# Two transformer blocks on one core: value rows centred before retention, the last down tile stacked in two parts, semaphores cleared in ranges

## The reference, cut to what matters

```python
def swiglu_ffn(x, w13, w2):
    a, u = jnp.split(x @ w13, 2, axis=-1)      # 2 x 2752 columns
    return (jax.nn.silu(a) * u) @ w2           # 2752 rows -> 1024

def retention(q, k, v, g, gn_g):               # 4 heads of 128, chunk-causal with decay
    ...
    mu = jnp.mean(o, axis=-1, keepdims=True)
    var = jnp.mean(jnp.square(o - mu), axis=-1, keepdims=True)
    o = ((o - mu) * lax.rsqrt(var + LN_EPS)).transpose(0, 2, 1, 3).reshape(B, L, D_RET) * gn_g
    return (jax.nn.silu(g.astype(f32)) * o).astype(g.dtype)

for l in range(DEPTH_2):
    h = layer_norm(DEEPNORM_ALPHA * h + 0.5 * swiglu_ffn(h, ffn1...), ...)
    mix = token_mix(h, w_in[l], ...)           # pooling, convolution, retention, then w_out
    h = layer_norm(DEEPNORM_ALPHA * h + mix, ...)
    h = layer_norm(DEEPNORM_ALPHA * h + 0.5 * swiglu_ffn(h, ffn2...), ...)
```

## Time and profile before

| | us |
|---|---|
| Runs shown (3) | 3224.69, 3225.98, 3226.51; median 3225.98 |
| The profiled execution | 3223.9, span 3222.1 |
| TensorE busy | 3138.6 (97%), granted clock 0.992 of full speed |
| VectorE, ScalarE, GpSimd busy | 973.9, 869.7, 1072.2 |
| "layers" begins | 1164.1 |
| Down products of the last group, first FFN of layer 0, begin | 1519.3 |
| Values of layer 0's mixer | 1658.4 to 1686.9 |
| Mixer's tail, layer 0 | 1719.2 to 1766.3 |
| Mixer's tail, layer 1 | 2737.5 to 2784.6 |

### The profile page before, as it was taken

How to read it: one execution, slowest core, us unless ns; L and a number is a source line. 1 busy time by engine, 2 the same in 40 slices (tenths; PEclk the granted TensorE clock), 3 DMA queues, 4 the chain that set the end, 5 groups by cost and what they waited for, 6 DMA issues and landing times.

```text
span 3222.1 us, 54521 instructions
## 1 busy us (share of the span) xinstructions
PE 3138.6 (97%) x23934; PEld 2553.9 (79%) x23934; DVE 973.9 (30%) x1762; ACT 869.7 (27%) x1304; POOL 1072.2 (33%) x563
## 2 busy tenths in 40 slices
PE   7999999989999989999999999999999999999998
PEld 3465578544444469999998999999999999888886
DVE  3144765531211241111463311113111254421113
ACT  2042423110000052222523522125221243252223
POOL 1030266200000034333563433344333355354442
PEclk9999999999999989999999999999999999999999
DMA  7541000349999942222221222222222222112220
GB/s 316 204 133 53 27 3 3 133 203 428 429 428 429 428 167 92 79 105 74 91 79 53 73 99 79 95 83 79 99 102 76 92 80 79 53 66 105 105 95 30
DMA packets 37752, 438.86 MB, mean 136 GB/s; under 512 B 5910, under 2 KB 6678, under 8 KB 11542
## 3 DMA queue, kind: packets, MB, share of 16 engines
q1 hardware_dynamic: 36088, 434.24, 34.2%
q10 hardware_dynamic: 1444, 1.36, 0.2%
HBM read 432.70 MB, written 2.10 MB: 135 GB/s over the span
## 4 chain that ended last, share of the span: by engine, by line
PE 62%; DVE 1%; ACT 0%; DVEq 0%; issue 0%; ACTq 0%
PE PS L2635 42%; PE PS L2632 11%; PE PS L2644 3%; PE PS L2909 2%; PE PS L2280 1%; PE PS L2942 1%; PE PS L2286 1%; PE PS L2927 1%; PE PS L2643 1%; PE PS L2293 0%; PE PS L2904 0%; DVE high L2385 0%; PE PS L2951 0%; DVE high L3229 0%; DVEq L2454 0%; DVE low L3223 0%
## 5 line engine op out<-in xcount | busy, mean ns | idle before, releaser
L2622 POOL TENSOR_TENSOR w_lo<-low,w_hi 128x2048 fp32r<-128x2048 f32 (+2 forms) x206 | 744.1, 3617 | 1565.5 <-ACT w_hi L2617 1565.1
L2635 PE MATMUL PS<-h_hi,w_hi 128*128 128x264 f32 x2656 | 553.8, 286 | 3.5 <-DVE h_lo L3254 3.4
L2635 PE MATMUL PS<-h_lo,w_hi 128*128 128x264 f32 x2656 | 552.1, 285 | 0.0
L2635 PE MATMUL PS<-h_hi,w_lo 128*128 128x264 f32 x2656 | 551.6, 285 | 0.0
L2617 ACT ACTIVATE w_hi<-low 128x2048 fp32r<-128x2048 f32 (+2 forms) x206 | 312.1, 1524 | 459.1 <-PE PS L2635 367.4
L2635 PEld LDWEIGHTS PS<-h_hi,w_hi 128*128 128x128 f32 x2656 | 417.3, 188 | 7.2 <-issue 6.2
L2635 PEld LDWEIGHTS PS<-h_lo,w_hi 128*128 128x128 f32 x2656 | 416.3, 188 | 0.0
L2635 PEld LDWEIGHTS PS<-h_hi,w_lo 128*128 128x128 f32 x2656 | 415.8, 188 | 0.0
L2772 DVE TENSOR_TENSOR low<-low,PS 128x528 f32<-128x528 f32 (+1 forms) x84 | 58.8, 699 | 778.0 <-PE PS L2635 556.3
L2635 PE MATMUL PS<-g_hi,w_hi 128*128 128x264 f32 x1056 | 231.9, 286 | 0.0
L2635 PE MATMUL PS<-g_hi,w_lo 128*128 128x264 f32 x1056 | 230.4, 285 | 0.0
(11 more groups left out here) (402 smaller groups left out, 4617.4 us busy)
## 6 DMA issues: line engine op xcount, KB each, us to landing
arena<-wts_dram SPq DMA_DIRECT2D x108, 2048.0 KB, 18.1
low<-wts_dram SPq DMA_DIRECT2D x70, 2048.0 KB, 7.7
arena<-wmod_dram SPq DMA_DIRECT2D x9, 2048.0 KB, 8.7
low<-wts_dram SPq DMA_DIRECT2D x12, 1536.0 KB, 6.4
arena<-na_bias_dram SPq DMA_DIRECT2D x16, 512.0 KB, 3.5
arena<-x_dram SPq DMA_DIRECT2D x2, 2048.0 KB, 8.2
high<-tab_dram SPq DMA_DIRECT2D x1, 2225.0 KB, 25.2
low<-wts_dram SPq DMA_DIRECT2D x2, 1024.0 KB, 5.1
```

The source lines that it names most:

```text
L2622: nc.gpsimd.tensor_tensor(lo, raw, hi.bitcast(F32), ALU.subtract).then_inc(w_l.sem, 1)
L2635: mm = nc.tensor.matmul(bank(b, h), w[wi], halves(x[xi])[:, h, :], start=(first and i == 0), stop=(last and i == 2))
```

## The change

Three edits. First, `clear` sorts the semaphore numbers and clears each consecutive run of them in one instruction; the order of instructions then has one clear at each of the three places instead of 50, 99 and 48.

Second, the last down tile is stacked. The host puts the 64 real rows a second time on partitions 64 to 127. GpSimd overwrites the last 128 columns of w_hi there with the low part of the weights (raw minus rounded), between two drains, and makes w_lo only for the other 896 columns. VectorE makes g on both halves of the partitions (a second multiply of 64 partitions, after a drain). The down products of this tile have two passes instead of three.

Third, the mean over a head's 128 values is taken from the values, not from the outputs: ScalarE evicts each value unit in two halves of 128 columns (one head each) with the sum over the columns as a second output, VectorE subtracts the mean from the value tile (`value_centre`, behind the convolution), and `values` waits for the centred tiles. `group_mean` and `group_centre` go; ScalarE squares the output straight from PSUM ahead of its copy. The tail's order is rewritten.

```diff
     def clear(self, sp):
-        for s in self.held:
-            sp.sem_clear(s)
+        at = sorted(s.num for s in self.held)
+        for i, n in enumerate(at):
+            if not i or at[i - 1] != n - 1:
+                first = n
+            if i + 1 == len(at) or at[i + 1] != n + 1:
+                sp.sem_clear(range(first, n + 1))
...
     def split_pool(pool, l, i):
         _, raw, hi, lo = piece(i)
         w_h.wait(pool, l, i + 1)
+        if i % NS in LAST_DOWN:
+            n, r = (GROUPS[-1][1] - 1) * P, slice(P // 2, P)
+            nc.gpsimd.drain()
+            nc.gpsimd.tensor_tensor(hi[r, n:], raw[r, n:], hi[r, n:].bitcast(F32), ALU.subtract)
+            nc.gpsimd.drain()
+            raw, hi, lo = raw[:, 0:n], hi[:, 0:n], lo[:, 0:n]
         nc.gpsimd.tensor_tensor(lo, raw, hi.bitcast(F32), ALU.subtract).then_inc(w_l.sem, 1)
+    LAST_DOWN = [w * S_FFN2 + S_FFN - DK + m for w in range(2) for m in range(DK)]
...
+    STACKED = ((0, 0), (0, 1))
...
-                                   range(2) if h is None else (h,))
+                                   range(2) if h is None else (h,), **(dict(pairs=STACKED) if f0 + f == FT - 1 else {}))
...
-                    x, r = gs[0:64, f % 2, :], slice(0, 64)
-                    nc.vector.tensor_tensor(toks(x, fin), toks(gs[64:128, f % 2, :], fin), sums(4, fin)[64:128], ALU.mult).then_inc(g_sb.sem, 1)
+                    x = gs[:, f % 2, :]
+                    nc.vector.tensor_tensor(toks(x[0:64], fin), toks(x[64:128], fin), sums(4, fin)[64:128], ALU.mult)
+                    nc.vector.drain()
+                    nc.vector.tensor_tensor(toks(x[64:128], fin), toks(x[64:128], fin), sums(4, fin)[64:128], ALU.mult).then_inc(g_sb.sem, 1)
...
             elif kind == "v":
-                c = 256 * (t // 5)
-                nc.scalar.activation(v[:, t % 5, c:c + 256], PS[:, b, 0:256], ACT.Copy).then_inc(u_a.sem, 1)
+                for x in range(2):
+                    at = 256 * (t // 5) + P * x
+                    nc.scalar.activation(v[:, t % 5, at:at + P], PS[:, b, P * x:P * x + P], ACT.Copy,
+                                         accum_out=vsum[:, 2 * t + x:2 * t + x + 1])
+                nc.scalar.drain().then_inc(u_a.sem, 1)
...
         def head_out(h):
             ro_ps.wait(act, l, h + 1)
+            if h >= 2:
+                gv_ps.wait(act, l, h - 1)
+            nc.scalar.activation(halves(sq2[h % 2]), PS[:, 4:6, 0:LH], ACT.Square).then_inc(gq_sb.sem, 1)
             nc.scalar.activation(halves(qT[:, h, :]), PS[:, 4:6, 0:LH], ACT.Copy).then_inc(ro_sb.sem, 1)
...
+        def value_centre(t):
+            taken(dve, l, "v", t)
+            x = v[:, t % 5, 256 * (t // 5):256 * (t // 5) + 256].rearrange("p (h n) -> p h n", h=2)
+            nc.vector.scalar_tensor_tensor(x, vsum[:, 2 * t:2 * t + 2].unsqueeze(2).to_broadcast([P, 2, P]), -1.0 / P, x,
+                                           ALU.mult, ALU.add).then_inc(vc_sb.sem, 1)
...
         convolve(len(taps))
+        for t in range(10):
+            value_centre(t)
...
+            m[DFF:] = m[DFF - P // 2:DFF]
```

More of the change, by code:

```diff
@@ L2190, in second_block @@
     u = M3.take(2, CW - 1 + L)
+    vsum = M3.take(20)
     acc, ropet, csq = (hT[:, 2 * i:2 * i + 2, :] for i in range(3))
@@ L2626, in weights, with product @@
         return piece(i)[2:]
-    def product(b, w, x, first, last, fin=False, hs=range(2)):
-        for i, (wi, xi) in enumerate([(0, 0), (0, 1), (1, 0)]):
+    def product(b, w, x, first, last, fin=False, hs=range(2), pairs=((0, 0), (0, 1), (1, 0))):
+        for i, (wi, xi) in enumerate(pairs):
+            ends = dict(start=(first and i == 0), stop=(last and i == len(pairs) - 1))
             if fin:
-                mm = nc.tensor.matmul(PS[:, b, :], w[wi], x[xi][:, NMETA:], start=(first and i == 0), stop=(last and i == 2))
+                mm = nc.tensor.matmul(PS[:, b, :], w[wi], x[xi][:, NMETA:], **ends)
                 continue
             for h in hs:
-                mm = nc.tensor.matmul(bank(b, h), w[wi], halves(x[xi])[:, h, :], start=(first and i == 0), stop=(last and i == 2))
+                mm = nc.tensor.matmul(bank(b, h), w[wi], halves(x[xi])[:, h, :], **ends)
         return mm
+    STACKED = ((0, 0), (0, 1))
     def first_three(pe, l, uu, i, fin=False):
@@ L2770, in ffn_dve @@
                 if f < FT - 1:
[L2771 removed]
+                    x = gs[:, f % 2, :]
                     nc.vector.tensor_tensor(toks(x, fin), toks(x, fin), sums(4 * (f % 2) + 2, fin), ALU.mult).then_inc(g_sb.sem, 1)
                 else:
[L2774 to L2775 removed]
+                    x = gs[:, f % 2, :]
+                    nc.vector.tensor_tensor(toks(x[0:64], fin), toks(x[64:128], fin), sums(4, fin)[64:128], ALU.mult)
+                    nc.vector.drain()
+                    nc.vector.tensor_tensor(toks(x[64:128], fin), toks(x[64:128], fin), sums(4, fin)[64:128], ALU.mult).then_inc(g_sb.sem, 1)
                 gh_sb.wait(dve, l, n + 1)
[L2777 removed]
+                nc.vector.tensor_tensor(toks(g_lo[:, f - f0, :], fin), toks(x, fin), toks(g_hi[:, f - f0, :].bitcast(F32), fin), ALU.subtract).then_inc(gl_sb.sem, 1)
             def evacuate(m, h=None, apart=4):
@@ L2837, in second_block @@
     st_ps, st_sb, ro_ps, ro_sb = Sig("st_ps", 4 * RH), Sig("st_sb", 4 * RH), Sig("ro_ps", RH), Sig("ro_sb", RH)
-    gm_ps, gc_sb, gq_sb, gv_ps, ge, gr, gi, gb_ps, gz, gy_sb = (Sig(x, RH) for x in (
-        "gm_ps", "gc_sb", "gq_sb", "gv_ps", "ge", "gr", "gi", "gb_ps", "gz", "gy_sb"))
+    gq_sb, gv_ps, ge, gr, gi, gb_ps, gz, gy_sb = (Sig(x, RH) for x in (
+        "gq_sb", "gv_ps", "ge", "gr", "gi", "gb_ps", "gz", "gy_sb"))
+    vc_sb = Sig("vc_sb", 10)
     wo_ps, wo_sb = Sig("wo_ps", NU_LN), Sig("wo_sb", NU_LN)
@@ L2933, in values @@
                 ro_sb.wait(pe, l, h)
+                gq_sb.wait(pe, l, h)
             else:
                 taken(pe, l, "pool", 1)
+            vc_sb.wait(pe, l, 5 + 5 * (h // 2))
             for hf in range(2):
@@ L2944, in values, with group_var @@
             last.then_inc(ro_ps.sem, 1)
-        def group_mean(h):
-            ro_sb.wait(pe, l, h + 1)
+        def group_var(h):
+            gq_sb.wait(pe, l, h + 1)
             if h >= 2:
                 gz.wait(pe, l, h - 1)
-            for hf in range(2):
-                last = nc.tensor.matmul(bank(GN_BANK[h], hf), C["mean_h"], halves(qT[:, h, :])[:, hf, :], start=True, stop=True)
-            last.then_inc(gm_ps.sem, 1)
-        def group_var(h):
-            gq_sb.wait(pe, l, h + 1)
             quads(GN_BANK[h], 0, sq2[h % 2], True, True, "mean_h").then_inc(gv_ps.sem, 1)
@@ L2984, in mix_pe @@
         st_sb.wait(pe, l, 4 * RH)
-        group_mean(1)
+        group_var(1)
+        out_part(0, range(0, 2))
         values(3)
-        group_mean(2)
-        group_var(1)
-        out_part(0, range(0, 4))
+        group_spread(1)
         group_var(2)
-        group_spread(1)
+        out_part(0, range(2, 4))
+        group_var(3)
         ro_sb.wait(pe, l, RH)
         out_part(1, range(0, 2))
-        group_mean(3)
         group_spread(2)
         out_part(1, range(2, 4))
-        group_var(3)
+        group_spread(3)
         for m in range(2):
             out_part(m, (4, 5))
-        group_spread(3)
         for k in (6, 7):
@@ L3062, in head_out @@
             ro_ps.wait(act, l, h + 1)
+            if h >= 2:
+                gv_ps.wait(act, l, h - 1)
+            nc.scalar.activation(halves(sq2[h % 2]), PS[:, 4:6, 0:LH], ACT.Square).then_inc(gq_sb.sem, 1)
             nc.scalar.activation(halves(qT[:, h, :]), PS[:, 4:6, 0:LH], ACT.Copy).then_inc(ro_sb.sem, 1)
-        def group_square(h):
-            gc_sb.wait(act, l, h + 1)
-            nc.scalar.activation(sq2[h % 2], qT[:, h, :], ACT.Square).then_inc(gq_sb.sem, 1)
         def group_root(h):
@@ L3086, in mix_act @@
         head_out(2)
-        group_square(1)
+        group_root(1)
         head_out(3)
-        group_square(2)
-        group_root(1)
         group_root(2)
         mixed_hi(4)
-        group_square(3)
-        mixed_hi(5)
         group_root(3)
-        mixed_hi(6)
-        mixed_hi(7)
+        for k in range(5, DK):
+            mixed_hi(k)
         for i in range(2, 6):
@@ L3211, in decayed @@
                 last.then_inc(st_sb.sem, 1)
-        def group_centre(h):
-            gm_ps.wait(dve, l, h + 1)
-            nc.vector.tensor_tensor(halves(qT[:, h, :]), halves(qT[:, h, :]), bank(GN_BANK[h]), ALU.subtract).then_inc(gc_sb.sem, 1)
         def group_eps(h):
@@ L3247, in mix_dve @@
         group_inverse(2)
-        group_centre(3)
+        group_eps(3)
         group_scale(2)
-        group_eps(3)
         group_inverse(3)
```

11 lines of the change are left out of this document (1 added, 10 removed).

## The result

| | before | after |
|---|---|---|
| median of the runs | 3226.24 us (3224.69 to 3226.93, 4 runs) | 3204.74 us (3202.56 to 3206.22, 4 runs) |
| profiled execution, its span | 3223.9, 3222.1 us | 3205.7, 3203.8 us |

The ratio is 0.9937 (95% interval 0.9924 to 0.9949): 21.5 us less by the medians, 18.3 by the two spans. Forecast were 3206.6 us and 19.4 us less. Later the changed kernel was timed again: 3204.71 us over 5 runs, ratio 0.994 (0.9927 to 0.9954), 19.5 us under the 3224.21 of the kernel before beside it.

A forecast was written before the change was run, and what follows sets the result against it. TensorE, busy 97% of the span, was taken to bound the kernel. Clears 2.6, stacked tile 7.8 and tails 9.0 sum to 19.4 us, from 3225.98 to 3206.6 us; range 3203 to 3212.

The forecast's parts named there:

- forecast case: Whole kernel: 19.4 us saved, median 3206.6 us; chance 0.79.
- Clears: Closing block before "layers": one clear instead of 48 saves 2.6 us; the 50 and 99 elsewhere give nothing.
- Stacked tile: Last down tile of the FFNs: fewer matmuls save 1.95 us in each of three, 1.9 in the final, 7.8 together.
- Cover on VectorE: Last FFN tile: g_lo ends at 1523.0 to 1523.4, before TensorE needs it at 1524.4; costs nothing.
- Rival B: Last FFN tile: g_lo or w_hi late, TensorE pays 1 us or so per FFN, 3210.6 us; chance 0.06.
- Cover on GpSimd: Last down pieces in the FFNs: 2.5 to 3.7 us each, hidden; GpSimd sets the pace only from 5.3 us.
- Values: Mixer's first part: evictions of 0.8 to 1.2 us, centrings of 0.4 to 0.8 us ending by 1690; costs nothing.
- Tail: Mixer's tail: dropped means and new order save 4.5 us per layer, 9.0 us in two layers.
- walk: Layer 0's mixer tail, followed event by event through the engines: a gain of 4.3 to 5.2 us.
- rival A: Mixer's tail gives nothing: the chain through three engines ends last, TensorE waits instead; 10.4 us remain, 3215.6 us; chance 0.09.
- Rival D: Mixer's tail: ScalarE's table load holds up the root by 1.4 us in the new order, 3209.4 us; chance 0.03.
- C: Last down products: GpSimd's pieces set the pace from 5.3 us each; at 8 us, 3250 us, slower; chance 0.03.

The follow-up runs named there:

- old-order run: The kernel before with only the centred values, means and subtractions gone, but its old tail order kept: 3220.35 us, ratio 0.9989 against the kernel before.

## Why the prediction was right

**Forecast 3206.6, measured 3204.74, inside the range of 3203 to 3212; 19.4 us of gain against 21.5 by the medians (19.5 when timed again) and 20.6 by the three stretches of the profile.** The forecast case held, none of the rivals.

- Clears: 2.6 forecast, 2.5 measured, with two clears left in the closing block and not one; the hidden 149 cost nothing.
- Stacked tile: 1.95 us for each FFN forecast, 1.98 measured. Cover on VectorE: g_lo at 1523.0 to 1523.4 forecast, 1523.35 measured. Rival B needs another 0.95 us there. Cover on GpSimd: it ends near 4.8 us a piece and not at 5.3.
- Values: eviction 0.8 to 1.2 us, measured 0.94. The centrings end at 1686.0 (1690 forecast); nine of them take 7.34 / 9 = 0.82 us each, just above my 0.4 to 0.8, and the tenth 0.43. Why they differ is open: GpSimd works beside the tenth too.
- Tail: this term was mis-sized, 4.5 us per layer against 5.1 measured, 9.0 against 10.2. The walk's bounds (4.3 to 5.2 us) held; what failed is the choice in it. Its places were right: spread 0 walked to 1737.1, measured 1736.9 on the same clock; spread 3 to 1753.95 or 1754.85, measured 1754.1; next product to 1761.1 or 1762.0, measured 1761.2. 4.5 lay near its later values, for which line 3229 had to take 1.67 us. All eight of the changed kernel take the short time:

```profile
L3240 DVE SCALAR_TENSOR_TENSOR high<-high x8: 767/769/769, 1736.8 to 2763.3; 128x528 f32<-128x528 f32 x8
```

- The walk had the new order's places right, but the text doesn't say that the gain hangs on it. It speaks of the means' 7.5 us and of waits that might swallow them; the old-order run shows that this is what would have happened (rival A in its mild form, 1.7 us a layer), and that the new order prevented it.
- Rival D: the root starts 0.02 us behind the table load (1732.15 + 1.28 to 1733.45), and not 1.4 us later, as the Trainium skill (ScalarE: Activation LUTs, What ACT_TABLE_LOAD costs) would have it.
- Rival A's mechanism was seen twice, in the old-order run and in the queue on VectorE; C's at 5.1 us a piece.

## What to carry over

When work is taken from the bound engine, walk the next chain before you count it: here 3.5 us of matmuls out of a tail gave 1.7 us in the old order and 3.5 in a new one, which alone gave 1.6; and a queue on VectorE that nobody had waited for was the next bound. Cover has a size: measure it by adding work to the hidden engine until the other one waits. And compare profiles from a common point behind the parts that were not touched, as the 3 us by which the untouched part came out longer here hid the 2.5 us that the clears gave.
